# A two-block model with a 32-expert layer: the routing stretch ahead of the experts is reordered

## The reference, cut to what matters

```python
h = layer_norm_2(DEEPNORM_ALPHA * h + y @ w_out, ln1_g, ln1_b)     # 256 x 1024
# moe(h): 32 experts, each token goes to 4
logits = h @ w_router + b_router                                    # 256 x 32
top_val, top_idx = top_k(logits, 4);  gates = softmax(top_val)
for e in range(32):                    # w_up[e]: 1024 x 2048, w_down[e]: 1024 x 1024, all float32
    hdn = h[tokens of e] @ w_up[e] + b_up[e]
    act = (clip(up) + 1) * min(gate, 7) * sigmoid(1.702 * gate)
    m[tokens of e] += gates * (act @ w_down[e] + b_down[e])
h = layer_norm_2(DEEPNORM_ALPHA * h + m, ln2_g, ln2_b)
h = h + sigmoid(h @ w_ple_gate + b_ple_gate) * (p @ w_ple)          # p @ w_ple: the "embedding"
```

## Time and profile before

| | us |
|---|---|
| median of 3 runs (lowest, highest) | 2378.13 (2377.28, 2379.11) |
| the profiled execution's own time | 2378.32 |
| its span in the trace | 2376.5 |
| PE busy | 2327.8 |
| DVE busy | 1189.4 |
| ACT busy | 835.6 |
| POOL busy | 192.8 |

### The profile page before, as it was taken

One profiled execution on the slowest core, in us unless ns is written; L12 is line 12 of the kernel. 1 busy time (PEld: TensorE's weight loads), 2 busy tenths in 40 slices (PEclk: granted clock), 3 DMA queues, 4 the chain that ended last, 5 costly groups with the idle time before them and its releaser, 6 DMA issues.

```text
span 2376.5 us, 33062 instructions
## 1 busy us (share of the span) xinstructions
PE 2327.8 (98%) x13409; PEld 1604.4 (68%) x13409; DVE 1189.4 (50%) x1621; ACT 835.6 (35%) x1028; POOL 192.8 (8%) x90
## 2 busy tenths in 40 slices
PE   9999999999999999999999999999999999999999
PEld 8889989888888998988899983333333333333335
DVE  5668766756755876675686772112211111111115
ACT  4554344544544434454448341111111111111113
POOL 0002502200200250220020000000000000000000
PEclk9999999999999999999999999999999999999999
DMA  8765454565556545456546689999999999999995
GB/s 271 235 203 175 150 188 146 180 204 180 195 185 206 176 145 192 144 178 203 185 144 197 204 314 407 428 427 428 428 425 429 427 427 427 427 428 428 427 425 229
DMA packets 222323, 666.37 MB, mean 280 GB/s; under 512 B 10099, under 2 KB 164339, under 8 KB 191620
## 3 DMA queue, kind: packets, MB, share of 16 engines
q1 hardware_dynamic: 222212, 664.77, 73.6%
HBM read 663.69 MB, written 1.05 MB: 280 GB/s over the span
## 4 chain that ended last, share of the span: by engine, by line
PE 80%; DMA 15%; SPq 4%; DVE 0%; issue 0%; ACT 0%; ACTq 0%; POOLq 0%; DVEq 0%
PE ps L829 17%; PE ps L790 13%; DMA ring<-in_w_up_dram 13%; PE ps L811 12%; PE ps L1426 9%; PE ps L817 6%; PE ps L1474 6%; PE ps L916 4%; SPq L483 2%; DMA work<-in_w_down_dram 2%; PE ps L1391 1%; PE ps L1400 1%; PE ps L1006 1%; PE ps L1632 1%; PE ps L1266 1%; PE ps L1058 1%
## 5 line engine op out<-in xcount | busy, mean ns | idle before, releaser
L2305 DVE TENSOR_TENSOR ring_halves<-ring,ring_halves 128x2048 fp32r<-128x2048 f32 (+1 forms) x214 | 527.1, 2473 | 190.0 <-ACT ring_halves L1732 189.7
L1732 ACT CAST ring_halves<-ring 128x2048 fp32r<-128x2048 f32 (+1 forms) x214 | 401.4, 1876 | 114.9 <-PE ps L829 90.4
L2886 DVE TENSOR_TENSOR work<-ps,work 128x256 f32<-128x256 f32 x64 | 26.9, 420 | 633.3 <-PE ps L1460 633.3
L811 PE MATMUL ps<-x_halves,ring_halves 128*128 128x512 f32 x1280 | 326.5, 392 | 0.1
L1426 PE MATMUL ps<-ring,work 128*64 128x512 f32 x1248 | 278.1, 595 | 24.0 <-DMA ring<-in_w_up_dram 24.0
L829 PE MATMUL ps<-ring_halves,work_halves 128*128 128x512 f32 x1184 | 288.7, 391 | 0.3
L790 PE MATMUL ps<-x_halves,ring_halves 128*128 128x256 f32 x2208 | 274.7, 285 | 0.1
L790 PEld LDWEIGHTS ps<-x_halves,ring_halves 128*128 128x128 f32 x2208 | 267.6, 192 | 2.1 <-issue 0.7
L811 PEld LDWEIGHTS ps<-x_halves,ring_halves 128*128 128x128 f32 x1280 | 230.2, 189 | 41.5 <-issue 0.5
L829 PEld LDWEIGHTS ps<-ring_halves,work_halves 128*128 128x128 f32 x1184 | 221.4, 188 | 48.7 <-issue 3.1
L1720 ACT COPY hT<-ps 128x512 f32<-128x512 f32 x96 | 56.2, 585 | 497.5 <-PE ps L1426 460.5
(11 more groups left out here) (294 smaller groups left out, 2447.9 us busy)
## 6 DMA issues: line engine op xcount, KB each, us to landing
ring<-in_w_up_dram SPq DMA_DIRECT2D x77, 2048.0 KB, 36.5
work<-in_w_up_dram SPq DMA_DIRECT2D x37, 2048.0 KB, 41.6
ring<-in_w_down_dram SPq DMA_DIRECT2D x36, 2048.0 KB, 40.4
ring<-in_w_in_dram SPq DMA_DIRECT2D x52, 1024.0 KB, 5.2
ring<-in_ffn_up_dram SPq DMA_DIRECT2D x44, 1024.0 KB, 5.4
ring<-in_ffn_down_dram SPq DMA_DIRECT2D x44, 1024.0 KB, 4.9
ring<-in_ffn_gate_dram SPq DMA_DIRECT2D x43, 1024.0 KB, 5.4
work<-in_w_down_dram SPq DMA_DIRECT2D x19, 2048.0 KB, 36.6
```

Of the source, the lines that this page charges most:

```text
L811: return pe.matmul(ps[:, b, :], high[:, o:o + P], x_both[:, :, k, :], start=(k == 0), stop=(k == DT - 1))
L1732: nc.scalar.copy(second_half(high_of(name)[:], name), second_half(ring[:, s, :], name))\
L2305: v.tensor_tensor(second_half(ring_halves[s][:], name), second_half(ring[:, s, :], name), second_half(high_of(name)[:].bitcast(F32), name) ...
```

## The change

- `wple_kept` is the memory of `hn`. Once both rows of `h` are made, ACT copies the embedding weights (128x2048) there. The copy's end and the end of product (0, 1) replace "rows" and (1, 1) in SP's wait for the pair (16, 17).
- The four embedding products of tile 1 move into the branches. In `few` one comes after the transposes of expert 0's rows, three after HEAD's `gate_up`. They read `wple_kept`.
- POOL makes `h` of both tiles; DVE's two operations for tile 1 are gone.
- `best` is cut in two: `highest(0)` runs ahead of tile 1's transposes' copies, `choose(0)`, `highest(1)`, `choose(1)` after them.
- `router(t)` takes each strip of `hT` as soon as ACT or DVE has made it, in the order 0, 4, 1, 5, 2, 6, 3, 7, and writes bank `t` in place of bank 2 * `t`.
- "gT", its copy, the copy of `BUP`, and the writing of `1.19 * h` into the result banks move into the branches, the last one into HEAD behind its `select`.

```diff
@@ SP, load_pair
                     sp.wait_ge(h_ready.sem, h_ready.at(("h", ("A",))))
-                    sp.wait_ge(dve_done.sem, dve_done.at("rows"))
-                    sp.wait_ge(pe_full.sem, pe_full.at(("ple", 1, 1)))
+                    sp.wait_ge(act_done.sem, act_done.at("wple kept"))
+                    sp.wait_ge(pe_full.sem, pe_full.at(("ple", 0, 1)))
@@ PE
             def router(t):
-                turned_copied(after, t)
-                open_bank(2 * t, ("router", t))
+                b = router_bank(t)
+                open_bank(b, ("router", t))
...
+                for k in (0, 4, 1, 5, 2, 6, 3, 7):
+                    if k % 4 == 3:
+                        evacuated(t_bank(after, t) + k // 4, ("T", after, t))
+                    else:
+                        by = dve_done if k > 3 else act_done
+                        pe.wait_ge(by.sem, by.at(("turned", t, k)))
...
+            def embedding(t, half, kk, branch=None):
...
+                if branch:
+                    pe.wait_ge(act_done.sem, act_done.at("wple kept"))
...
             router(0)
             embedding(0, 0, 0)
             transposes(after, 1, hn)
+            router(1)
             embedding(0, 0, 1)
+            counts(0)
             embedding(0, 1, 0)
-            router(1)
+            counts(1)
             embedding(0, 1, 1)
-            counts(0)
-            embedding(1, 0, 0)
-            counts(1)
-            embedding(1, 0, 1)
@@ PE, step(ph) of few
                     gate_up(ph)
+                    if ph == HEAD:
+                        for half, kk in ((0, 1), (1, 0), (1, 1)):
+                            embedding(1, half, kk, "few")
+                        for b in range(4, 8):
+                            emptied[b].add("rows in")
@@ PE, few
                 rows_turned("xg0", "xgt0")
+                gates_by_expert("few")
+                embedding(1, 0, 0, "few")
                 step(HEAD)
@@ PE, ahead of the branch
             pe.wait_ge(h_ready.sem, h_ready.at(("h", ("A",))))
-            pe.wait_ge(dve_done.sem, dve_done.at("rows"))
             pe.wait_ge(sel_ready.sem, sel_ready.at("sel0"))
             gather_rows("xg0")
-            embedding(1, 1, 0)
-            embedding(1, 1, 1)
-            open_bank(3, "gT")
-            pe.wait_ge(dve_done.sem, dve_done.at("gates"))
-            full(pe.transpose(ps[:, 3, 0:P], w(GATES4, P), ident[:]), "gT")
             pe.wait_ge(dve_done.sem, dve_done.at("most"))
@@ ACT, behind the norm
-            act.wait_ge(tables.sem, tables.at("all"))
-            done(nc.scalar.copy(w(BUP, 512), w(BUPROWS, 512)), "bup")
-            embedded(0, 1)
-            mine("bup")
-            embedded(1, 0)
+            act.wait_ge(h_ready.sem, h_ready.at(("h", ("A",))))
+            done(nc.scalar.copy(wple_kept, w(V, 2 * D)), "wple kept")
@@ ACT, few
                 columns_back("xgt0")
-                last_embedded()
+                embedded(0, 1)
+                gates_kept("few")
+                biases_kept("few")
                 step(HEAD)
@@ DVE
-            def second_rows():
-                mine(("hn", ("A",), 1))
-                dve.wait_ge(lnp_in.sem, lnp_in.at((("A",), 1)))
-                done(v.tensor_tensor(h[:, 1, :], hn[:, 1, :], w(LNP["A"], D), ALU.mult), "scaled")
+            def first_highest():
                 dve.wait_ge(tables.sem, tables.at("all"))
+                highest(0)
-            ln(("A",), ("ln1_g_2", "ln1_b_2"), 0, ALPHA2, second_rows)
-            done(best(0), ("chosen", 0))
-            done(best(1), ("chosen", 1))
-            mine("scaled")
-            done(v.tensor_tensor(h[:, 1, :], h[:, 1, :], w(LNP["A"] + D, D), ALU.add), "rows")
+            ln(("A",), ("ln1_g_2", "ln1_b_2"), 0, ALPHA2, first_highest)
+            choose(0)
+            highest(1)
+            choose(1)
@@ POOL, residual
-                for t in range(1 if tag[0] == "A" else TT):
+                for t in range(TT):
...
-                    if t == 1 or tag[0] == "A":
+                    if t == 1:
                         ins.then_inc(h_ready.add(("h", tag)), 1)
```

More of the change, by code:

```diff
@@ L415, in gate_high_free, with router_bank @@
                         slot_used(eng, weight(i, what, k))
+        def router_bank(t):
+            return t
+        wple_kept = hn[:].rearrange("p t n -> p (t n)")
         gut = hT[:].rearrange("p k t -> p (k t)")
@@ L1307, in router, with gates_by_expert @@
             def router(t):
-                turned_copied(after, t)
-                open_bank(2 * t, ("router", t))
-                pe.matmul(ps[:, 2 * t, 0:32], ones[0:1, :], brout[0:1, :], start=True, stop=False)
-                for k in range(DT):
-                    mm = pe.matmul(ps[:, 2 * t, 0:32], hT[:, k, t * P:t * P + P], w(ROUTER + k * 32, 32),
+                b = router_bank(t)
+                open_bank(b, ("router", t))
+                pe.matmul(ps[:, b, 0:32], ones[0:1, :], brout[0:1, :], start=True, stop=False)
+                for k in (0, 4, 1, 5, 2, 6, 3, 7):
[4 more added lines that the diff above has]
+                        pe.wait_ge(by.sem, by.at(("turned", t, k)))
+                    mm = pe.matmul(ps[:, b, 0:32], hT[:, k, t * P:t * P + P], w(ROUTER + k * 32, 32),
                                    start=False, stop=(k == DT - 1))
                 full(mm, ("router", t))
-            def embedding(t, half, kk):
+            def embedding(t, half, kk, branch=None):
                 b = acc_bank(after, t) + half
                 if kk == 0:
-                    open_bank(b, ("ple", t, half))
-                mm = pe.matmul(ps[:, b, :], w(PTURN + kk * T + t * P, P), w(V + kk * D + half * 512, 512),
-                               start=(kk == 0), stop=(kk == 1))
-                if kk == 1:
-                    full(mm, ("ple", t, half))
+                    open_bank(b, ("ple", t, half, branch) if branch else ("ple", t, half))
+                if branch:
+                    pe.wait_ge(act_done.sem, act_done.at("wple kept"))
+                c = kk * D + half * 512
+                mm = pe.matmul(ps[:, b, :], w(PTURN + kk * T + t * P, P),
+                               wple_kept[:, c:c + 512] if branch else w(V + c, 512), start=(kk == 0), stop=(kk == 1))
+                if kk == 1:
+                    full(mm, ("ple", t, half, branch) if branch else ("ple", t, half))
+            def gates_by_expert(branch):
+                open_bank(3, ("gT", branch))
+                pe.wait_ge(dve_done.sem, dve_done.at("gates"))
+                full(pe.transpose(ps[:, 3, 0:P], w(GATES4, P), ident[:]), ("gT", branch))
             pe.wait_ge(ple_in.sem, ple_in.at("wple"))
@@ L1360, in expert_biases @@
             def expert_biases():
-                evacuated(3, "gT")
+                evacuated(3, ("gT", "many"))
                 pe.wait_ge(bias_in.sem, bias_in.at("bdown"))
@@ L1544, in last_step @@
                     last_down((1, 2, 3))
-                for b in range(4, 8):
-                    emptied[b].add("rows in")
                 rows_turned("xg0", "xgt0")
+                gates_by_expert("few")
+                embedding(1, 0, 0, "few")
                 step(HEAD)
@@ L1594, in step @@
                     pe.wait_ge(dve_done.sem, dve_done.at((ph, "act", 3)))
+                gates_by_expert("many")
+                for half in range(2):
+                    for kk in range(2):
+                        embedding(1, half, kk, "many")
                 expert_biases()
@@ L1749, in evac_T @@
                                                bias=col(gname[1], i + k), scale=col(gname[0], i + k))
+                    if tag == ("A",) and k < 3:
+                        done(ins, ("turned", t, k))
                 ins.then_inc(emptied[b].sem, 1)
@@ L2121, in _, with embedded, gates_kept @@
             ln(("A",), ("ln1_g_2", "ln1_b_2"), 0)
-            def embedded(t, half):
-                pe_group(("ple", t, half))
+            def embedded(t, half, branch=None):
+                pe_group(("ple", t, half, branch) if branch else ("ple", t, half))
                 copy_out(acc_bank(("A",), t) + half, w(PLE + t * D + half * 512, 512))
+            def gates_kept(branch):
+                pe_group(("gT", branch))
+                nc.scalar.copy(w(GT, P), ps[:, 3, 0:P]).then_inc(emptied[3].sem, 1)
             for t in range(TT):
@@ L2134, in _, with biases_kept @@
                     embedded(0, 0)
-            act.wait_ge(tables.sem, tables.at("all"))
-            done(nc.scalar.copy(w(BUP, 512), w(BUPROWS, 512)), "bup")
-            embedded(0, 1)
-            mine("bup")
-            embedded(1, 0)
[L2141 to L2144, removed]
+            act.wait_ge(h_ready.sem, h_ready.at(("h", ("A",))))
+            done(nc.scalar.copy(wple_kept, w(V, 2 * D)), "wple kept")
+            def biases_kept(branch):
+                act.wait_ge(tables.sem, tables.at("all"))
+                done(nc.scalar.copy(w(BUP, 512), w(BUPROWS, 512)), ("bup", branch))
```

(39 more changed lines are left out.)

4 lines of the change are left out of this document (2 added, 2 removed).

## The result

The changed kernel takes 2383.0 us (10 runs, 2380.58 to 2384.73) against 2377.74 (2376.59 to 2379.25) for the one before: a ratio of 1.0023, 95% interval 1.0014 to 1.0032, or +5.3 us. Forecast was +2.6, with a range that ended at 2382.7.

A forecast was written before the change was run, and what follows sets the result against it. The load stream bounds the end. Expert 1 starts 1.8 + 2.6 - 0.7 = 3.7 us later, so the 2.6 us hole closes and one of 5.2 opens: +2.6, forecast 2380.7 us, range 2376.4 to 2382.7.

The forecast's parts named there:

- The bound: Expert stage: it cannot end sooner than its stream of weight loads, 403 MB or 943 us at 428 GB/s.
- SP's release by 1430.5, the hole closed: SP's load of pair (16, 17): issued before the queue is dry at 1432.5, removing a DMA idle worth 2.6 us.
- HEAD longer by 2.6: HEAD, between its `gate_up` and its gather: three embedding products that nothing covers add 2.6 us.
- Between gather and HEAD, -0.7: From the end of expert 0's gather to HEAD's `gate_up`: 2.4 us in place of 3.2, taken as -0.7.
- The routing chain, g = +1.8: Routing up to expert 0's gather: DVE's small operations wait for POOL's whole instructions, so selection ends 1.8 us later.
- rival A: Routing chain: DVE waits for POOL only once; g = +0.4, expert 1 +2.3, time 2379.3 us; chance 0.25.
- router(1) by strips: Routing chain: taking strips as they come gains nothing, since the late strips are DVE's.
- the counts come 0.7 us after `chosen`: Routing chain: DVE's next instruction needs PE's counts, put at 0.7 us after `chosen`, with expert 0's selection 0.5 later.
- B: Routing chain: DVE's small operations never wait for POOL; g = -2.1, time 2376.4 us in the middle; chance 0.15.
- C: Branch ahead of HEAD: it loses its cover and must fetch code, +3.9 us on top, 2384.6; chance 0.05.
- D: SP's wait for (16, 17): not over before 1432.5 as POOL's operations take 8 us; 2381 to 2383; chance 0.03.

The follow-up runs named there:

- e1: Changed kernel with three additional matmul products on TensorE in the routing stretch, results overwritten; 2379.17 us against 2378.02 for the kernel before, ratio 1.0007.
- e4: e1 with HEAD's three embedding products cut to two matmuls of 32 columns, most of tile 1's embedding left out; 2377.03 us, ratio 0.9997 to the kernel before.
- b3: Kernel before with two embedding products moved from ahead of router(1) to behind it, nothing else changed; 2380.79 us against 2377.21, ratio 1.0011.
- e2: Changed kernel with tile 1's rows made by VectorE as before, POOL making only tile 0's; 2381.65 us, ratio 1.0014 to the kernel before.

## Why the prediction was wrong, point by point

- *The bound.* Right. The loads' idle time follows the time of every kernel above. (403 MB at 428 GB/s are 941 us, not 943; nothing rests on it.)
- *SP's release by 1430.5, the hole closed.* Wrong by the clock: 1432.27. In e1 the hole is gone (430 GB/s from 1432 to 1434). The copy of 2048 columns takes 1.90 us, estimated 2.
- *HEAD longer by 2.6.* `gate_up` to `gate_up` is 22.47 us in e1 and in the changed kernel, 19.47 before: +3.0. The six matmuls take 2.84 by their row; e4 gets 2.2 of it back with two small matmuls left.
- *Between gather and HEAD, -0.7.* In e1 4.33 in place of 5.11, -0.8: right. In the changed kernel 5.38, +0.3.
- *The routing chain, g = +1.8.* VectorE's chain took rival A's times (`choose(0)` done at 1425.1, A had 1425.4; `choose(1)` at 1427.2, A had 1427.4), though not its single wait: the cast and `choose(0)` both wait, and the negation, which the forecast had waiting, does not. At full clock g is 0.0 in e1 (gather at 1428.61), where A had +0.4. The nearest row, two numbers per partition, was the wrong guide for one number.
- *The step that failed.* In this g, every matmul had its duration of before. It was said that router(1) by strips "is worth nothing here" and that the counts come 0.7 us after `chosen`. I took four products out of the stretch, put two others behind router(1), let TensorE wait for strips, and did not ask what that does to its clock: its cost stood at nothing in the sum, with no reason given. The clock fell to 0.50 for some 10 us. The counts came 2.0 us later than VectorE could take them (its wait for L1357), the last product before the gather took 2.05 in place of 1.10, the gather 2.98 in place of 1.94. e1 shows this at 4.1 us of the 5.3. Without it the forecast's terms err by +1.8 (g) and -0.4 (HEAD).
- *Rivals.* e1, at full clock, came to +1.2, as A had it, in part by luck: g 0.4 too high and HEAD 0.4 too low cancel. B is excluded by the cast's 1.73 us, C by HEAD's start in e1. D's late issue nearly came (1432.27), but not in D's way: POOL's two operations took 2.35 us each. Slower by more than 0.2% had a chance of 0.07, and for reasons other than this one.

The Trainium skill, page "SBUF — State Buffer", section "Who interferes with whom", has the exclusive pair of ports. This trace agrees: 1.73 against 0.17 us for a cast of eight numbers, 1.24 against 0.24 for 32, no wait where the input is in `ps`. The Trainium skill's page "VectorE: DVE Perf Modes", section "What auto-detection actually checks", lets a single source and a destination in SBUF use both ports where their outermost non-unit dimensions are both even or equal. A single number per partition has no such dimension, and the section does not speak of that case; here it took 0.15 us beside POOL, as it does alone.

Left open: how the fall of the clock divides between the gap ahead of router(1) and the lighter stretch behind it. b3 has the gap alone and is down for about 3 us, the changed kernel has both and stays down for some 10, e2, with fewer products but no wait for POOL, for about 7. What the kernel before would gain at most from this stretch is also not shown beyond the 2.7 us of its lost loads.

## What to carry to other kernels

Where a stream of loads ends last, add up its idle time before and after a change: here that gave the change within 1.1 us in eleven kernels, and engine times were only reasons for it. Work that fills an engine's waits may be what keeps its clock up; before taking matmuls out of a stretch with small matmuls and gaps, price the stretch at half clock as well. A two-engine split of small operations is worth little where one engine's long operation makes the other's short ones wait for its end.

## What the runs showed of the hardware

- The granted clock fell from 1.00 to 0.50 although TensorE never stood still for more than 1.75 us at a time (b3) or 1.0 us (the changed kernel); from 1418 to 1424, at whose end or soon after it fell, TensorE was busy for 4.25 and 4.81 us of the 6 (5.11 in e2), against 5.97 in the kernel before, which kept it.
- Three products of waste work took 4 us off the changed kernel, by the medians.
- A cast of eight numbers per partition waited until the end of the POOL operation under way (1.73 and 1.74 us in place of 0.17, beside one of 2.35 us); an operation on one number did not (0.15 us).
- A 2 MB load on a drained or nearly drained queue landed 8.3 us (changed kernel, 1432.27) to 9.3 us (b3, 1436.14) after its issue; 2097 KB at 428 GB/s are 4.9 of these.
